# FFN gated values of groups one to ten turned by DMA as 16-bit planes instead of by TensorE

## The reference, cut to what matters

```python
h = h + attention(rms_norm(h)) @ w_o
h = h + (silu(n @ w_gate) * (n @ w_up)) @ w_down     # n = rms_norm(h); w_down is 2816 x 1024
h = h + sigmoid(rms_norm(h) @ ple_w_gate) * (p @ ple_w_proj)
```

## Time and profile before

| | |
|---|---|
| Median of 3 runs | 1340.85 us (1340.55 to 1340.93) |
| Profiled execution, its own time | 1340.77 us |
| Its span | 1339.0 us |
| TensorE's mean granted clock | 1.000 |
| Moved by DMA | 240.33 MB, mean 179 GB/s |

### The profile page before, as it was taken

The page is one execution under the profiler, slowest core; times in us unless marked ns, Lnnn a source line. Parts: engine busy times, 40 slices in busy tenths (PEclk is TensorE's granted clock), DMA queues, the critical chain, the costliest instruction groups (busy, mean ns, idle before and its releaser), DMA issues.

```text
span 1339.0 us, 20732 instructions
## 1 busy us (share of the span) xinstructions
PE 1326.4 (99%) x6870; PEld 1106.2 (83%) x6870; DVE 922.5 (69%) x1618; ACT 778.0 (58%) x1411; POOL 114.2 (9%) x179
## 2 busy tenths in 40 slices
PE   9999999999999999999999999999999999999998
PEld 7987888888898788888888888888887778888887
DVE  7887665557887665555698875555677887655565
ACT  7666555546765655554675565555478766555544
POOL 6030332200000000000010000000002210000000
PEclk9999999999999999999999999999999999999999
DMA  9444877766554555655644456555545545555661
GB/s 334 138 161 127 230 222 219 217 193 195 168 167 140 157 181 187 187 186 193 211 134 158 126 180 188 188 186 188 200 158 182 174 134 165 190 187 188 188 203 49
DMA packets 143999, 240.33 MB, mean 179 GB/s; under 512 B 11906, under 2 KB 102193, under 8 KB 143936
## 3 DMA queue, kind: packets, MB, share of 16 engines
q1 hardware_dynamic: 140928, 230.47, 53.8%
q0 software_dynamic: 2832, 8.49, 3.1%
q10 hardware_dynamic: 176, 0.54, 0.2%
HBM read 238.33 MB, written 1.13 MB: 179 GB/s over the span
## 4 chain that ended last, share of the span: by engine, by line
PE 92%; DVE 5%; ACT 1%; issue 1%; DMA 1%; POOL 0%; SPq 0%; DVEq 0%; ACTq 0%
PE acc L1481 14%; PE acc L1483 14%; PE acc L1482 14%; PE sc L1483 11%; PE sc L1481 11%; PE sc L1482 11%; PE turn L1642 5%; PE acc L1592 3%; PE acc L1594 2%; PE acc L1593 2%; DVE wlo L1047 2%; PE turn L1738 1%; PE sc L1695 1%; DVE z L1144 1%; PE turn L1722 1%
## 5 line engine op out<-in xcount | busy, mean ns | idle before, releaser
L1047 DVE SCALAR_TENSOR_TENSOR wlo<-raw,aT_gain,whi 128x512 fp32r<-128x512 f32 (+2 forms) x612 | 430.2, 758 | 24.4 <-ACT whi L762 24.4
L762 ACT ACTIVATE whi<-raw,aT_gain 128x512 fp32r<-128x512 f32 (+2 forms) x612 | 405.0, 723 | 29.7 <-PE acc L1483 23.5
L1481 PE MATMUL sc<-whi,xhi 128*128 128x512 f32 x640 | 252.7, 395 | 0.0
L1483 PE MATMUL sc<-whi,xlo 128*128 128x512 f32 x640 | 249.6, 390 | 0.0
L1482 PE MATMUL sc<-wlo,xhi 128*128 128x512 f32 x640 | 249.3, 390 | 0.0
L1481 PE MATMUL acc<-whi,xhi 128*128 128x512 f32 x432 | 173.4, 401 | 1.1 <-DVE wlo L1047 0.8
L1483 PE MATMUL acc<-whi,xlo 128*128 128x512 f32 x432 | 168.7, 390 | 0.0
L1482 PE MATMUL acc<-wlo,xhi 128*128 128x512 f32 x432 | 168.4, 390 | 0.0
L1045 DVE TENSOR_TENSOR wlo<-raw,whi 128x1024 fp32r<-128x1024 f32 x120 | 141.9, 1217 | 0.0
L1483 PEld LDWEIGHTS sc<-whi,xlo 128*128 128x128 f32 x640 | 120.1, 188 | 25.3
L1294 DVE SCALAR_TENSOR_TENSOR aT_gain<-sc,rstd,aT_gain 128x256 f32<-128x256 f32 x80 | 38.7, 484 | 147.4 <-ACT aT_gain L895 147.4
(11 more groups left out here) (206 smaller groups left out, 2001.6 us busy)
## 6 DMA issues: line engine op xcount, KB each, us to landing
raw<-in_ffn_w_gu SPq DMA_DIRECT2D x176, 256.0 KB
raw<-in_qk SPq DMA_DIRECT2D x62, 512.0 KB
raw<-in_ffn_w_gate SPq DMA_DIRECT2D x88, 256.0 KB
raw<-in_ffn_w_up SPq DMA_DIRECT2D x88, 256.0 KB
raw<-in_ffn_w_down SPq DMA_DIRECT2D x44, 512.0 KB
raw<-in_ffn_w_d SPq DMA_DIRECT2D x44, 512.0 KB
raw<-in_ple_w_gate SPq DMA_DIRECT2D x32, 512.0 KB
raw<-in_da_w_qkv SPq DMA_DIRECT2D x8, 512.0 KB
```

Of the source, the lines that this page charges most:

```text
L762: ins = act.activation(whi[:, u % RING, c0:c1], raw[:, u % RING, c0:c1], ACT.Copy, scale=scale)
L1047: ins = dve.scalar_tensor_tensor(out=lo, in0=w, scalar=gain[:, g:g + 1], in1=hi.bitcast(F32), op0=ALU.mult, op1=ALU.subtract)
L1481: pe.matmul(dst, xh, wh, start=first, stop=False)
L1483: return pe.matmul(dst, xl, wh, start=False, stop=last)
```

## The change

Gated values of groups 0 to 9 of each layer no longer go through TensorE. VectorE copies the upper and the lower 16 bits of each number into two planes (`split_planes`), right behind `hidden`; SyncE issues two DMA transposes of 128 partitions x 512 16-bit numbers a group, one for each tile of 128 rows (`turn_planes`); ScalarE writes the turned halves back side by side into `joined_g` (two copies), and makes `ghi` from it (one copy); VectorE makes `glo` from `joined_g` and `ghi`. ScalarE and VectorE do this at b = 3 where they did it at b = 1. SyncE has no wait of its own for the planes: VectorE waits for them before the weights' split that follows, and SyncE's next load waits for that split. So the transposes stand behind the load of unit b = 1 of the next body but one (b = 3 for the first group, and behind the last down unit for the tenth). Group 10 is turned by TensorE as before. The table gathers of layer 0 wait for unit b = 3 of their body, not b = 0.

```diff
+        planes = aT[:, 0, 512:1024].bitcast(U16).rearrange("p (t h c) -> p t h c", t=T, h=2)
+        planes_t = aT[:, 1, 512:1024].bitcast(U16).rearrange("p (h k s) -> p h k s", h=2, k=2)
+        halves_16 = aT[:, 1, 0:512].bitcast(U16).rearrange("p (t c h) -> p t c h", t=T, h=2)
+        joined_g = z[:, 0, 0:512]
@@ SyncE @@
-                with sp.Fori(0, NG - 1) as i:
+                def turn_planes():
+                    for t in range(T):
+                        sp.dma_start_transpose(planes_t.rearrange("p h k s -> p (h k) s")[:, :, t * P:(t + 1) * P],
+                                               planes[:, t].rearrange("p h c -> p (h c)")).then_inc(planes_turned, 16)
+                def ffn_body(i, turned):
                     for b in range(4):
                         u = base + U_FFN + b
                         load(u, gu_parts(L, u, b, i * GC_COLS + GC_COLS), i)
+                        if b == turned:
+                            turn_planes()
...
+                ffn_body(0, None)
+                ffn_body(1, 3)
+                with sp.Fori(2, NG - 1) as i:
+                    ffn_body(i, 1)
...
                 for b in range(2):
                     u = base + U_DOWN_LAST + b
                     load(u, [(raw[:, u % RING, :], rows(down_w[L], 2 * (NG - 1) + b, 0, D), 2)])
+                turn_planes()
@@ GpSimd @@
-                        pool.wait_ge(unit_done, U_FFN + 6 * n + 1)
+                        pool.wait_ge(unit_done, U_FFN + 6 * n + 4)
@@ ScalarE, ffn_body @@
-                        if b == 1:
-                            for t in range(T):
-                                e = EV[("g", L, 0, t)]
-                                act.wait_ge(turned, i * 2 + (e + 1))
-                                act.activation(ghi[:, :, t * P:(t + 1) * P],
-                                               tb[e % 2][:, 0:256].rearrange("p (k c) -> p k c", k=2),
-                                               ACT.Copy).then_inc(turn_hi, 1)
+                        if b == 3:
+                            act.wait_ge(planes_turned, i * 32 + 32 * (dma_groups(L) + 1))
+                            if not isinstance(i, int) or i:
+                                act.wait_ge(g_lo, i + dma_groups(L))
+                            for h in range(2):
+                                ins = act.activation(joined_g.bitcast(U16).rearrange("p (c h) -> p c h", h=2)[:, :, 1 - h],
+                                                     planes_t[:, 1 - h].rearrange("p k s -> p (k s)"), ACT.Copy)
+                            ins.then_inc(g_joined, 1)
+                            act.wait_ge(g_joined, i + (dma_groups(L) + 1))
+                            act.wait_ge(unit_done, i * 6 + (base + U_FFN))
+                            act.activation(ghi, joined_g.rearrange("p (k s) -> p k s", k=2), ACT.Copy).then_inc(g_hi, 1)
@@ VectorE @@
+            def split_planes(done):
+                dve.wait_ge(gu_out, done)
+                for h in range(2):
+                    ins = dve.tensor_copy(planes[:, :, h, :], halves_16[:, :, :, h])
+                ins.then_inc(planes_ready, 1)
...
                 hidden(L, acc, 2 * NG * L)
+                split_planes(2 * NG * L + 2)
@@ VectorE, ffn_body @@
-                        if b == 1:
-                            for t in range(T):
-                                e = EV[("g", L, 0, t)]
-                                at = (slice(None), slice(None), slice(t * P, (t + 1) * P))
-                                lo_half(("g", L, 0, t), glo[at], ghi[at],
-                                        tb[e % 2][:, 0:256].rearrange("p (k c) -> p k c", k=2), e, i, 2)
+                        if b == 3:
+                            dve.wait_ge(g_hi, i + (dma_groups(L) + 1))
+                            dve.tensor_tensor(glo, joined_g.rearrange("p (k s) -> p k s", k=2), ghi.bitcast(F32),
+                                              ALU.subtract).then_inc(g_lo, 1)
...
                         if b == 4:
                             hidden(L, [sc[:, t, :] for t in range(T)], 2 * NG * L + 2, i, 2)
+                            if not peeled:
+                                split_planes(i * 2 + (2 * NG * L + 4))
+                                dve.wait_ge(planes_ready, i + (dma_groups(L) + 2))
...
+                dve.wait_ge(planes_ready, dma_groups(L) + 1)
                 with dve.Fori(0, NG - 2) as i:
@@ TensorE @@
-                        if b == 1:
-                            turn_g(L, 0, 2 * NG * L, i)
                         gu_unit(L, U_FFN + b, b, i)
@@ TensorE, down_unit @@
                 if b == 0:
-                    for t in range(T):
-                        e = EV[("g", L, g, t)]
-                        pe.wait_ge(turn_out[e % 2], turns + (e // 2 + 1))
+                    if g == NG - 1:
+                        for t in range(T):
+                            wait_out(pe, EV[("g", L, g, t)])
+                    else:
+                        pe.wait_ge(g_lo, turns + (dma_groups(L) + 1))
```

More of the change, by code:

```diff
@@ L24 @@
 F32R = mybir.dt.float32r
+U16 = mybir.dt.uint16
 BF16 = mybir.dt.bfloat16
@@ L50, with dma_groups @@
 AHEAD = RING - 2
+def dma_groups(L):
+    return (NG - 1) * L
 X_PARTS = [(0, 2), (2, 4), (4, 6), (6, 8)]
@@ L245, in turn_events @@
                     ev.append(("o", L, j))
-            if U_FFN <= s < U_DOWN_LAST and (s - U_FFN) % 6 == 1:
-                ev += [("g", L, (s - U_FFN) // 6, t) for t in range(T)]
             if s == U_DOWN_LAST - 1:
@@ L385, in build @@
         gated = sem("gated")
+        planes_ready, planes_turned = sem("planes_ready"), sem("planes_turned")
+        g_joined, g_hi, g_lo = sem("g_joined"), sem("g_hi"), sem("g_lo")
         qk_hi, qk_lo, qk_bias_in = sem("qk_hi"), sem("qk_lo"), sem("qk_bias_in")
@@ L970, in _, with ffn_body @@
                 hidden_sig(L, 1, acc[1])
-                def ffn_body(i, peeled):
+                def ffn_body(i, last=False):
                     for b in range(6):
-                        if b == 1:
-                            for t in range(T):
-                                e = EV[("g", L, 0, t)]
-                                act.wait_ge(turned, i * 2 + (e + 1))
-                                act.activation(ghi[:, :, t * P:(t + 1) * P],
-                                               tb[e % 2][:, 0:256].rearrange("p (k c) -> p k c", k=2),
-                                               ACT.Copy).then_inc(turn_hi, 1)
-                        if peeled and b == 5:
+                        if b == 3:
[9 more added lines that the diff above has]
+                            act.activation(ghi, joined_g.rearrange("p (k s) -> p k s", k=2), ACT.Copy).then_inc(g_hi, 1)
+                        if last and b == 5:
                             for t in range(T):
@@ L993, in ffn_body @@
                             hidden_sig(L, 1, sc[:, 1, :])
-                        if peeled:
+                        if last:
                             split_ahead(L, U_FFN + 6 * i + b)
@@ L1000, in _ @@
                 with act.Fori(0, NG - 2) as i:
-                    ffn_body(i, False)
-                ffn_body(NG - 2, True)
+                    ffn_body(i)
+                ffn_body(NG - 2, last=True)
                 for s in range(U_DOWN_LAST, UNITS):
@@ L1747, in attention, with turn_g @@
                     turn(e, [o[:, t, k * P:(k + 1) * P] for k in range(2) for t in range(T)])
-            def turn_g(L, g, wait, turns=0):
+            def turn_g(L):
                 for t in range(T):
-                    e = EV[("g", L, g, t)]
-                    use(e, turns)
-                    pe.wait_ge(gu_out, turns * 2 + (wait + t + 1))
+                    e = EV[("g", L, NG - 1, t)]
+                    use(e)
+                    pe.wait_ge(gu_out, 2 * NG * (L + 1) - T + t + 1)
                     turn(e, [aT[:, 1, t * 256 + k * P:t * 256 + (k + 1) * P] for k in range(2)])
@@ L1843, in ffn_body @@
                         if last and b == 1:
-                            turn_g(L, NG - 1, 2 * NG * L + 2 * (NG - 1))
+                            turn_g(L)
                         down_unit(L, U_FFN + 4 + b, b, 0, first and b == 0, None, i)
```

## The result

The changed kernel takes **1328.88 us** (median of 4 runs, 1328.60 to 1329.24) against 1340.82 for the kernel before (4 runs): a ratio of 0.9911, 95% interval 0.9899 to 0.9923, that is 11.9 us less. Forecast were 1331.2 us and a range of 1321 to 1350. The profiled execution took 1329.14 us with a span of 1327.3 us, so the spans differ by 1339.0 - 1327.3 = 11.7 us.

The account below looks back on a forecast made before the run. TensorE, busy 99% of the span, was taken to bound the kernel. 1340.77 us less 19.2 for the turns removed plus 9.6 for TensorE's stands in each layer's first group gave 1331.2 us, range 1321 to 1350.

Parts of the forecast that it names:

- Removed: On TensorE, forty turns of gated values at 0.48 us each go away: -19.2 us, all on the path.
- The rest hidden in the steady state: In groups after a layer's first, the added copies, joins and DMAs make nothing wait at X = 4.7 us.
- X: Time from the issue of a group's first DMA transpose to the landing of the second: 4.7 us, ends 2.4 and 7.7.
- The stand before each first down unit: TensorE waits in each layer's first group, 2.5 us in three layers and 2.1 in layer 2: +9.6 us.
- The window I gave: In each layer's first group, time from first transpose issue to the landing needed: 2.2 us, 2.6 in layer 2.
- The slower rival: Transposes land later than 7.1 us, so later groups take 9.2 + X: 1417 us at X = 9.0; chance 0.27.
- 9.2 + X: Loop through ScalarE's in-order work in each steady-state group; must stay under 16.3 us, so X up to 7.1.
- I cost the move at nothing: Layer 0's table gathers, moved from unit 1 to unit 4 of a group, cost 0 us, covered by slack.

Follow-up runs that it names:

- e1: The changed kernel with each layer's first transposes issued as soon as the planes are ready, ahead of the load of unit 9: 1321.88 us.
- e9: e1 with TensorE also turning the gated values of groups one to ten at the old place, result unread: 1341.17 us.
- e6: e1 with two more pairs of transposes ahead of the real pair in groups two to ten: 1396.67 us.
- e8: e1 with the table gathers of layer 0 back behind the first unit of a group: 1333.67 us.
- e7: The changed kernel with the gathers' DMAs back behind a group's first unit, but GpSimd's additions held until unit 4 is done: 1334.55 us.
- e2: The changed kernel with the table gathers of layer 0 back behind the first unit of a group: 1338.58 us.
- e10: e1 with the table gathers back behind a group's first unit, except the first piece, which stays behind the fourth: 1328.29 us.
- e5: e1 with one more pair of transposes ahead of the real pair in groups two to ten: 1323.92 us.
- e4: The changed kernel with TensorE also turning the gated values of groups one to ten at the old place, result unread: 1350.61 us.

## Why the prediction was right

**Removed: right.** 19.2 us of turns; 19.0 from e1 and 19.3 from e9.

**The rest hidden in the steady state: right, with mis-sized terms.** A SyncE issue of a transpose takes 1.25 us and not 0.37, which I had taken from the loads. The issue of both, 2.5 us, is thus most of X. The landing of one, 3.1 us median from its issue (2.5 to 3.9), is less than the 4.3 I took from loads. The two errors go opposite ways, and X came out at 3.8 to 4.3 against 4.7: that it was so near is in part luck. The two copies to planes take 0.76 us together and not 1.2. VectorE's 10.86 and ScalarE's 9.91 us of a group are what I worked out (11.0 and 10.0).

**The stand before each first down unit: right in place and kind,** 7.2 us with the slow restart against 9.6. The window I gave, 2.2 us (2.6 in layer 2), was met: to be in time the pair would have to land by 145.5 in layer 0 and by 797.75 in layer 2 (2.85 us ahead of the down unit's place), and it leaves at 143.30 and 795.07, 2.2 and 2.7 us earlier. Here too errors cancel: the copies are 0.4 us shorter, and hand-overs that I did not count cost about as much (0.22 us of them is VectorE waiting for its own copies). So the term that was mis-sized is X: it is 0.4 to 0.9 us less in each of the four layers, and these are 2.8 of the 3.0 us between 9.6 and the 6.6 found. The restart, 0.6 us, was not in the sum. With it this term is 2.4 us too high, and the turns gave 19.0 and not 19.2: that is the distance of 2.3 us between forecast and result.

**The slower rival: its mechanism right, its condition not met.** 9.2 + X was the period in e6 (18.27 us at X = 9.1). In the changed kernel no transpose landed later than 3.9 us from its issue, so that X is 5.2 us at most, under the 7.1 that this rival needs. The Trainium skill's table in VectorE: DVE Perf Modes, The three transpose paths (1309 ns for a 128x128 16-bit block) does not add up block by block here: eight blocks in two DMAs were there 3.9 us after the first issue, where 8 x 1309 ns would be an estimated 10.5 us.

**"I cost the move at nothing": right for the move as made, but one of its two reasons fails.** The first reason holds: in the changed kernel the gather begins 5.0 us ahead of the transposes (166.92 and 171.91 in one group), and ScalarE joins at 176.25 without having waited for them. The second, that slack would cover it (7.1 less 4.7, 2.4 us), does not: a gather close to the pair lengthens X from 3.9 to as much as 9.2 us in e8, more than all the slack. The move is cheap because it avoids the meeting. The prediction did not say what the change would be worth without it, and that is 9.7 us less.

## What to carry to other kernels

Work can be taken off a full TensorE by a longer path through other engines and DMA if each use of the result has slack for the whole path; count that slack per use, since the first use after a prologue can have two units less than all the others, and put the transfer's issue at its data, not behind the next load. A loop through in-order engines has a period of its own (here 9.2 us + X); know it, as nothing shows in the time until it passes TensorE's. Before another queue's transfers are moved or left, look at what they will meet. And when an experiment holds some work back, look in its trace where that work lands instead: in e7 it landed on the splits that it was meant to spare.

## What the runs showed of the hardware that I had not expected

- A DMA transpose of 128 x 512 16-bit numbers holds the issuing engine 1.25 us (1197 to 1313 ns, 80 times), a weights' load of 256 KB 0.37 us.
- A pair of transposes that is done in 3.7 to 3.9 us took 5.8 to 9.2 when a gather of four 128 KB DMAs was issued 0.25 to 1.9 us behind it (e2, e8, e10). The strip above shows the DMA engines busy and slow, not idle.
- How long TensorE stood does not alone decide whether its granted clock fell. It stayed at 1.00 (2.4 GHz) behind the changed kernel's stands of 1.4 to 1.6 us, behind one of 2.10 in e5 and one of 3.08 in e6. It fell behind those of 2.76 (e4), 3.07 (e10), 4.68 (e7), 4.74 (e8) and 4.82 (e2), and also behind one of 1.89 in layer 3 of e7 (columns of the stretch as above):

```profile
1142.20 0.52 PE L1525 MATMUL acc<-whi,split_qg 128*128 128x512 f32 x1 [1.89 <-DVE split_qg L1473]
```

```profile
1144.00:1148.00 4.00, 4.00 (x15) 3.18 (x14) 3.84 (x9) 2.88 (x4) 0.00 (x0) 0.75 0.41 131
```

- A fall meant seven to twelve starts 0.43 us apart instead of 0.23: 1.4 us lost in e2 and e4, 1.6 to 2.4 in e7, e8 and e10.
- GpSimd's additions beside VectorE's splits slow both. In e7, where they run together, two additions took up to 3.47 us and six splits 6.14 to 6.16; apart they take 2.54 and 4.06. In the changed kernel two additions took up to 5.3 us.
